# Scatters between the two rows of a chunk's products, and one multiplication on GpSimd, in a decoder step with 32 experts

## What is computed

```python
def hierarchical_moe(x, g_ffn, w_rg, b_rg, w_re, b_re, w_gate, w_up, w_down):
    xn = rmsnorm(x, g_ffn).reshape(bsz * L, D_MODEL)
    ...                                   # grp: best of 4 groups; top 2 of its 8 experts; combine: their weights
    out = jnp.zeros_like(xn)
    for g in range(N_EXPERT_GROUPS):
        h = jax.nn.silu(jnp.einsum('nd,edf->nef', xn, w_gate[g])) * jnp.einsum('nd,edf->nef', xn, w_up[g])
        out = out + jnp.einsum('nef,efd->nd', h * combine[:, g, :, None], w_down[g])
    return x + out.reshape(bsz, L, D_MODEL)
...
y_prompt = rmsnorm(h_p, g_final)          # rmsnorm(x, g) = x * rsqrt(mean(x * x) + EPS) * g
y_sample = rmsnorm(h_s, g_final)
```

## Time and profile before

| | us |
|---|---|
| median of the runs | 1584.56 |
| time of the profiled execution | 1587.11 |
| its span, first to last instruction | 1585.4 |
| PE busy | 1335.9 (84%) |
| DVE busy | 556.2 (35%) |
| ACT busy | 407.3 (26%) |
| POOL busy | 20.5 (1%) |
| chain that ended last | PE 60%, DMA 37%, DVE 1%, issue 1% |

### The profile page before, as it was taken

One profiled execution on the slowest core, in us unless ns is written; L12 is line 12 of the kernel. 1 busy time (PEld: TensorE's weight loads), 2 busy tenths in 40 slices (PEclk: granted clock), 3 DMA queues, 4 the chain that ended last, 5 costly groups with the idle time before them and its releaser, 6 DMA issues.

```text
span 1585.4 us, 24042 instructions
## 1 busy us (share of the span) xinstructions
PE 1335.9 (84%) x9971; PEld 915.0 (58%) x9971; DVE 556.2 (35%) x898; ACT 407.3 (26%) x623; POOL 20.5 (1%) x54
## 2 busy tenths in 40 slices
PE   9999999999999999999778578578487487497497
PEld 8999999999999999962322222232232232232232
DVE  6657765554455555432112112012012021021024
ACT  6545343333333343332101102002002002002003
POOL 0000000000000000010000000000000000000000
PEclk9999999999999999999979789789789699699699
DMA  9777445545545769799999999999999999999997
GB/s 370 286 271 279 159 160 187 186 159 192 181 183 185 263 239 384 286 396 412 437 433 437 434 428 440 437 425 440 435 427 442 428 430 441 433 429 436 429 429 295
DMA packets 40697, 544.68 MB, mean 344 GB/s; under 512 B 5561, under 2 KB 7737, under 8 KB 13505
## 3 DMA queue, kind: packets, MB, share of 16 engines
q1 hardware_dynamic: 40360, 543.96, 83.9%
q10 hardware_dynamic: 288, 0.04, 0.0%
HBM read 540.30 MB, written 3.68 MB: 343 GB/s over the span
## 4 chain that ended last, share of the span: by engine, by line
PE 60%; DMA 37%; DVE 1%; issue 1%; ACT 0%; SPq 0%; DVEq 0%; ACTq 0%
DMA ring<-in_expert_chunks 37%; PE bank L1663 12%; PE bank L1664 12%; PE bank L1665 12%; PE bank L2131 7%; PE bank L2134 4%; PE bank L1990 3%; PE bank L2049 1%; PE bank L2041 1%; PE bank L1982 1%; PE bank L1922 1%; PE bank L1924 0%; PE bank L1923 0%; PE bank L1698 0%; PE bank L1700 0%
## 5 line engine op out<-in xcount | busy, mean ns | idle before, releaser
L1152 DVE TENSOR_TENSOR w_lo<-ring,w_hi 128x1024 fp32r<-128x1024 f32 x216 | 255.9, 1226 | 225.3 <-ACT w_hi L855 224.7
L1663 PE MATMUL bank<-xn_hi,w_hi 128*128 128x264 f32 x1120 | 318.9, 285 | 0.0
L1664 PE MATMUL bank<-xn_lo,w_hi 128*128 128x264 f32 x1120 | 317.3, 283 | 0.0
L1665 PE MATMUL bank<-xn_hi,w_lo 128*128 128x264 f32 x1120 | 317.1, 283 | 0.0
L855 ACT ACTIVATE w_hi<-ring 128x1024 fp32r<-128x1024 f32 x216 | 217.1, 1052 | 373.9 <-PE bank L1665 318.0
L1663 PEld LDWEIGHTS bank<-xn_hi,w_hi 128*128 128x128 f32 x1120 | 210.9, 188 | 1.5 <-issue 1.4
L1664 PEld LDWEIGHTS bank<-xn_lo,w_hi 128*128 128x128 f32 x1120 | 211.0, 188 | 0.1
L2131 PE MATMUL bank<-side 128*32 128x512 f32 x1024 | 130.8, 648 | 94.2 <-DMA side<-in_expert_chunks 94.1
L1665 PEld LDWEIGHTS bank<-xn_hi,w_lo 128*128 128x128 f32 x1120 | 210.0, 187 | 0.0
L2131 PE MATMUL bank<-ring,side 128*32 128x512 f32 x752 | 101.3, 661 | 90.7 <-DMA ring<-in_expert_chunks 90.6
L1563 DVE TENSOR_SCALAR side<-bank,small 128x128 f32<-128x128 f32 x56 | 19.6, 351 | 373.7 <-PE bank L1990 373.7
(11 more groups left out here) (333 smaller groups left out, 1580.1 us busy)
## 6 DMA issues: line engine op xcount, KB each, us to landing
ring<-in_dense_units SPq DMA_DIRECT2D x108, 1024.0 KB, 4.8
ring<-in_expert_chunks SPq DMA_DIRECT2D x27, 4096.0 KB, 22.9
trunk<-in_expert_chunks SPq DMA_DIRECT2D x13, 4096.0 KB, 35.0
ring<-in_expert_chunks SPq DMA_DIRECT2D x14, 2048.0 KB, 11.7
side<-in_expert_chunks SPq DMA_DIRECT2D x4, 4096.0 KB, 30.6
side<-in_expert_chunks SPq DMA_DIRECT2D x5, 2048.0 KB, 10.7
trunk<-in_expert_chunks SPq DMA_DIRECT2D x5, 2048.0 KB, 16.2
ring<-in_expert_chunks SPq DMA_DIRECT2D x5, 1024.0 KB, 8.6
```

The source lines that it names most:

```text
L1152: V.tensor_tensor(w_lo[n % 2][:, js, :], raw[n % 2][:, js, :], w_hi[n % 2][:, js, :], ALU.subtract).then_inc(lo_done, 1)
L1663: mm(ps[:, 0:n], w_hi[b][:, j, :], x_hi[:, j, :], start=j == k0, stop=False)
L1664: mm(ps[:, 0:n], w_hi[b][:, j, :], x_lo[:, j, :], start=False, stop=False)
L1665: ins = mm(ps[:, 0:n], w_lo[b][:, j, :], x_hi[:, j, :], start=False, stop=j == k1 - 1)
```

## The change

The three scatters of a round no longer stand ahead of chunks 18, 20 and 22 but between the two rows of their products. And the product of the samples' first 1024 columns with the norm's weights, the third instruction of line 1603, goes from VectorE to GpSimd: VectorE gives a signal (`rows_added`) ahead of its own two, GpSimd waits for it as its last instruction, and ScalarE's scaling of the samples waits for GpSimd (`gs_done`).

```diff
@@ -417,6 +417,7 @@
         even_turned, even_taken = sem("even_turned"), sem("even_taken")
         y_final, ya_final, fin_ready, fin_sq = (
             sem("y_final"), sem("ya_final"), sem("fin_ready"), sem("fin_sq"))
+        rows_added, gs_done = sem("rows_added"), sem("gs_done")
 
         def raw_count(n, g=0):
 
@@ -833,6 +834,8 @@
             pool.wait_ge(p_step, 3)
             G.tensor_tensor(Pw, P01, combx[:, :, 0:EPR].unsqueeze(3).to_broadcast([P, 3, EPR, CAP]), ALU.mult).then_inc(p_ready, 1)
             G.tensor_copy(combx[:, :, NX:NX + EPR], combx[:, :, 0:EPR]).then_inc(comb_ok, 1)
+            pool.wait_ge(rows_added, 1)
+            G.tensor_tensor(acc(2, 0, 1024), acc(2, 0, 1024), like(2, g_sb[S0:S0 + TS, 0:1024]), ALU.mult).then_inc(gs_done, 1)
 
         @block.scalar
         def _(act):
@@ -1117,6 +1120,7 @@
             act.wait_ge(f_rms, 2)
             nc.scalar.activation(acc2[:, 1, 1024:1536], acc2[:, 1, 1024:1536], ACT.Copy, scale=rx[:, 1:2]).then_inc(ya_final, 1)
             act.wait_ge(f_rms, 3)
+            act.wait_ge(gs_done, 1)
             nc.scalar.activation(acc(2, 0, 1536), acc(2, 0, 1536), ACT.Copy, scale=rx[S0:S0 + TS, 2:3]).then_inc(ya_final, 1)
 
 
@@ -1599,8 +1603,9 @@
                 V.tensor_scalar(cidx, cidx, float(CAP), None, ALU.add).then_inc(cidx_step, 1)
                 dve.wait_ge(cidx_step, k + 1)
 
-            for t, (p0, p1, _, _) in enumerate(ACC):
-                V.tensor_tensor(acc(t, 0, 1024), acc(t, 0, 1024), like(t, g_sb[p0:p1, 0:1024]), ALU.mult)
+            dve.nop().then_inc(rows_added, 1)
+            for t in range(2):
+                V.tensor_tensor(acc(t, 0, 1024), acc(t, 0, 1024), g_sb[:, 0:1024], ALU.mult)
             dve.wait_ge(sq_done, npass * (9 * ROUNDS) + 1)
             link(V.tensor_reduce(ss_most, ssh4[:, :, 0:3], AX.X, ALU.add))
             V.tensor_scalar(ss_most, ss_most, EPS, None, ALU.add).then_inc(f_var, 1)
@@ -2079,8 +2084,6 @@
                     if c == 17:
                         pe.wait_ge(p_step, it + 4)
                         gather(0, it * JPR, JOB_NEXT)
-                    if c in (18, 20, 22):
-                        scatter((c - 18) // 2)
                     if c == 19:
                         pe.wait_ge(aux_done, it * JPR + (A_E + JOB_LATE + 3))
                         last_columns(0)
@@ -2114,6 +2117,8 @@
                             pe.wait_ge(first_taken, 2)
                         elif jj and c < 8:
                             pe.wait_ge(aux_done, it * JPR + (A_E + c + 1))
+                        if jj and c in (18, 20, 22):
+                            scatter((c - 18) // 2)
                         if jj and c == CPR - 1:
                             for half, arrived in enumerate((half_full, quarter_full)):
                                 pe.wait_ge(arrived, it * 16 + 16)
```

## The result

| | before | after |
|---|---|---|
| median of 22 runs each, us | 1584.32 (1582.65 to 1586.83) | 1586.35 (1585.75 to 1588.51) |
| time of the profiled execution, us | 1587.11 | 1587.54 |
| its span, us | 1585.4 | 1585.8 |
| DVE busy, POOL busy, us | 556.2, 20.5 | 557.0, 22.5 |

A forecast was written before the change was run, and what follows sets the result against it. The prediction took the middle rounds as bound by the weight stream and the end as set by VectorE. Its terms, +1.19 - 1.22 + 1.70 = +1.67 us, on 1584.56 gave 1586.2 us, range 1583.9 to 1588.2.

The forecast's parts named there:

- The middle rounds cost nothing: Middle rounds: chunks given back 2.94 us later, but queued transfers and TensorE's next 14.69 us wait absorb it; cost 0.
- The wait for chunk 22 becomes bare, and the third scatter comes 1.19 us later: Last round, TensorE: third scatter no longer covers chunk 22's landing at 1566.5, so it starts at 1567.46, +1.19 us.
- The instruction gone from VectorE, -1.22: Tail on VectorE: one multiplication fewer there, saving 1.22 us.
- GpSimd's stall, 1.70: Tail: GpSimd's multiplication holds one of VectorE's two 128x1024 ones, +1.70 us, possible 0 to 3.85; chance 0.55.
- TensorE's path doesn't decide: Tail: TensorE ends 0.23 us later with 0.61 us to spare, so VectorE's path sets the end.
- No stall: Rival, tail: GpSimd costs VectorE nothing, total -0.03 us, 1584.5 us; chance 0.24.
- A tail bound by TensorE: Rival, last round: chunk 22 lands by 1563.9, all three waits saved, 1580.9 us, or 1582.6 with GpSimd's stall; chance 0.06.
- The fall of the clock: Rival, last round: TensorE's clock falls at the bare wait for chunk 22, 1.69 us more, 1587.9 us; chance 0.12.
- if chunk 22 lands before 1565: Sign of being wrong, last round: chunk 22 landing before 1565, where 1566.5 was expected.

The follow-up runs named there:

- first round alone: Against the kernel before: scatters moved between the rows in the first round only, nothing given to GpSimd; 1584.12 us, ratio 0.9997.
- the scatters alone: Against the kernel before: all three scatters of a round moved as in the change, all three multiplications kept on VectorE; 1586.27 us, ratio 1.0016.
- the third one alone: Against the kernel before: only the third scatter moved, between the rows of chunk 22, nothing given to GpSimd; 1585.63 us, ratio 1.0012.
- the first two alone: Against the kernel before: only the scatters at chunks 18 and 20 moved between the rows, nothing given to GpSimd; 1583.11 us, ratio 0.9995.
- harmless GpSimd: Two variants of the change: GpSimd fills zeros instead of multiplying (ratio 1.0002), or multiplies beside VectorE's PSUM-operand multiplications (ratio 1.0002); both against before.
- late signal: The change with VectorE's separate signal to GpSimd placed behind its two 128x1024 multiplications; 1587.14 us, ratio 1.0016 against the kernel before.
- GpSimd alone: Against the kernel before: only the samples' multiplication moved to GpSimd, all scatters left ahead of their chunks; 1585.04 us, ratio 1.0007.
- GpSimd writes only: The change with GpSimd filling the samples' 8x1024 with zeros instead of multiplying; 1585.25 us, ratio 1.0002 against the kernel before.
- both beside PSUM: GpSimd's multiplication released beside VectorE's PSUM-operand multiplications, against before: first two scatters moved, 1582.80 us, ratio 0.9989; all three moved, 1584.61 us, ratio 1.0002.

## Why the prediction was right, step by step

The time was forecast at 1586.2 and measured at 1586.35. That the two lie so near is in part luck: the forecast added 1.67 to a median of 1584.56, and 2.03 was measured beside 22 runs of before with a median of 1584.32. By its steps:

- **The middle rounds cost nothing.** Right, as forecast to the size: rate 433 GB/s, the wait of 14.69 shorter by 3.07. From the pair that lands at 1087.5 before and 1085.7 after to the landing of chunk 22 both kernels take 479.0 us. The first round too (first round alone, 0.9997).
- **The wait for chunk 22 becomes bare, and the third scatter comes 1.19 us later.** Right: 1.86 us idle ahead of the first half; 1.3 us more from landing to end with the scatters alone, the same with the third one alone, and 0.8 us less with the first two alone.
- **The instruction gone from VectorE, -1.22.** Right, and bare only where nothing stalls: 18.8 to 19.0 us with the scatters and a harmless GpSimd (two kernels), 20.2 with the scatters alone.
- **GpSimd's stall, 1.70.** The term that was mis-sized: it measured 2.20. The prediction scaled the 0.959 us of one instruction of line 1152 by the elements, and took GpSimd to come in behind VectorE's first. It came first, by 0.02 us, and VectorE stood for nearly all of its 2.36. The order hardly mattered (where GpSimd came in behind VectorE's first, with the late signal, VectorE's second took 3.374, 2.15 more than alone); the length of GpSimd's instruction was what the scaling had too small. The nearer measure stood in the earlier trace rows: line 834, with VectorE idle, took 0.832 us for 384 elements, which makes 2.22 for 1024. That GpSimd's instruction lies on 8 partitions only did not spare VectorE. With 2.20 the sum is +1.19 - 1.22 + 2.20 = +2.17, against 2.2 by landing to end and 2.03 by the medians. (The estimate of 2.2 from the Trainium skill, page "GPSIMD Engine Reference", section "Elementwise — side-by-side cycle accounting", was the nearer one.)
- **TensorE's path doesn't decide.** Right: ScalarE's squares began at 1574.86, released by VectorE, and the reciprocal followed VectorE's own work. Chunk 23 ended 6.3 us behind chunk 22's landing before and 6.7 after, 0.4 later (forecast 0.23).
- **The rivals.** No stall is excluded by the 3.424 us row; it is what GpSimd's fill gave. A tail bound by TensorE needed the landing to come before 1563.9 with the others as they were; it landed at 1564.7 in an execution whose TensorE was earlier too, and waited. The fall of the clock is real but not the rule: of the six profiled executions with all three scatters between the rows, one has it at the bare wait for chunk 22 and one at that for chunk 20 (late signal: 1.94 us for the first half, 3.77 for the scatter, after 2.25 us of wait). Its price in the first is 1.53 us on the scatter (forecast 1.69 with the first half).

One of its own signs of being wrong came: "if chunk 22 lands before 1565". It landed at 1564.7, where the prediction had 1566.5, and with it the first half of chunk 22 (1564.72) and the end of chunk 23 (1571.4, not near 1573.0) came 1.6 to 1.8 us early; the bare wait was 1.86 us, not 2 to 2.5. What the sum needs is a bare wait for chunk 22, and there was one, because TensorE came early as well. The sign was badly chosen: executions of kernels with before's middle rounds land chunk 22 at 1563.1 (GpSimd alone), 1566.4 (first round alone) and 1566.5 (before).

One thing the prediction took for granted and got away with: it made its sum against one execution, in which the clock had fallen at 1540.54 and TensorE lay 1.7 us back. Without the fall the kernel before takes 17.6 us from landing to end, and the late scatter costs 20.2 - 17.6 = 2.6 us, not 1.3. How often the kernel before runs in the one way or the other isn't known. Of the fourteen profiled executions of all kernels here, eight have that fall in the last round behind the same two pauses of 0.97 and 0.78 us (before, all scatters, GpSimd alone, third alone, first two alone, GpSimd writes only, and both beside PSUM) and six don't. If the kernel before has it as often, a rough estimate of the late scatter's cost is 8/14 x 1.3 + 6/14 x 2.6 = 1.9 us (somewhat less, since in GpSimd alone the third scatter began 0.36 us behind an early landing and could lose only 0.6); the medians of the scatters alone give 2.0 (by its ratio 1.1 to 4.0). That +1.19 came near the measured time for the whole is thus in part luck as well, and that part stays open.

## What to carry to other kernels

Work that stands ready while a transfer is awaited belonged ahead of that wait here, even with an idle piece of its own: the first two scatters could move without a loss, and the third cost 1.3 us or more. Before an instruction is handed to a second engine to save 1.2 us, ask which instructions of the first will stand beside it and through which memory both read; the same instruction cost 2.2 us beside two-SBUF multiplications, 2.2 beside a scalar addition on 128x3, and nothing beside multiplications from PSUM. And count a tail from the event that it hangs on, in several executions, rather than from the start of the span.

## What the runs showed of the hardware

- A signal on an instruction that does nothing else passed VectorE's queued multiplications: GpSimd started 0.16 us after the first of two had begun, 2.2 us before the pair would have ended. A signal on the result came 0.08 us after the second's end (1569.16 to 1569.24).
- A 128x3 scalar addition stood for the whole of GpSimd's instruction, 2.35 us for 0.17. Multiplications with an operand in PSUM were not touched (687 to 694 ns).
- A GpSimd memset of 8x1024 took 0.95 us and held nothing; the multiplication of the same size took 2.36.
- The weight stream lands chunk 22 anywhere from 1562.7 to 1566.5 in single executions of these kernels, a spread larger than the effect of any edit here, at 432 to 434 GB/s over 870 to 1100 us in all of them. It is there by 1090 us: in twelve of the thirteen other kernels the distance in time to before's trace changes by no more than 0.1 us from the pair that lands there to chunk 22.
